# Wide inverse square roots of a two-block transformer kernel: square root and VectorE reciprocal, or ScalarE exp of minus half the logarithm

## What is computed

```python
def rms_norm(x, w):
    xf = x.astype(jnp.float32)
    y = xf * lax.rsqrt(jnp.mean(xf * xf, axis=-1, keepdims=True) + NORM_EPS)
    return (y * w.astype(jnp.float32)).astype(x.dtype)

def l2norm(x):                       # q and k of the delta net
    return x * lax.rsqrt(jnp.sum(x * x, axis=-1, keepdims=True) + NORM_EPS)

# RWKV-7: the removal keys, and the norm of each head's output
kk = kk * lax.rsqrt(jnp.maximum(jnp.sum(kk * kk, axis=-1, keepdims=True), 1e-24))
y = ((y - mu) * lax.rsqrt(var + GN_EPS)).reshape(bsz, s, c) * gn_w + gn_b
```

## Time and profile before

| | |
|---|---|
| median of 3 runs | 2821.63 us |
| profiled execution, its own time | 2820.33 us |
| its span in the trace | 2818.5 us |
| TensorE busy | 2771.2 us (98%) |
| VectorE busy | 2023.7 us (72%) |
| ScalarE busy | 1364.0 us (48%) |
| GpSimd busy | 479.3 us (17%) |
| mean granted TensorE clock | 0.997 of full speed |

### The profile page before, as it was taken

How to read it: one execution, slowest core, us unless ns; L and a number is a source line. 1 busy time by engine, 2 the same in 40 slices (tenths; PEclk the granted TensorE clock), 3 DMA queues, 4 the chain that set the end, 5 groups by cost and what they waited for, 6 DMA issues and landing times.

```text
span 2818.5 us, 42260 instructions
## 1 busy us (share of the span) xinstructions
PE 2771.2 (98%) x16660; PEld 2434.1 (86%) x16660; DVE 2023.7 (72%) x3102; ACT 1364.0 (48%) x2051; POOL 479.3 (17%) x526
## 2 busy tenths in 40 slices
PE   8999999999999999999999999999999999999998
PEld 7888888888888888888888888878998888888887
DVE  7987797776776666656657888878677777667655
ACT  6453455455555445434435545434454444444434
POOL 2211011110111111001102635421111111001101
PEclk9999999999999999999999999999999999999999
DMA  6444333455555555555556534221365555555555
GB/s 227 162 160 159 121 116 132 145 191 188 193 187 190 192 191 191 192 190 193 188 183 199 177 124 133 92 76 53 120 202 191 191 192 189 193 188 194 189 180 164
DMA packets 133396, 474.65 MB, mean 168 GB/s; under 512 B 14800, under 2 KB 15056, under 8 KB 132944
## 3 DMA queue, kind: packets, MB, share of 16 engines
q1 hardware_dynamic: 133200, 471.96, 50.3%
HBM read 469.80 MB, written 2.10 MB: 167 GB/s over the span
## 4 chain that ended last, share of the span: by engine, by line
PE 90%; DVE 5%; ACT 2%; POOL 1%; issue 1%; DMA 0%; SPq 0%; DVEq 0%; ACTq 0%; POOLq 0%
PE ps L899 90%; DVE U L1869 1%; DVE ringl L1869 1%; POOL U L2551 1%; ACT high L1409 1%; PE ps L902 1%; POOL U L2624 0%; ACT U L1409 0%; DVE U L1878 0%; DVE xT L1869 0%; DMA xT<-in_x_dram 0%; DVE hx L1869 0%; DVE U L2067 0%; ACT hr L1409 0%; DVE U L1875 0%
## 5 line engine op out<-in xcount | busy, mean ns | idle before, releaser
L899 PE MATMUL ps<-hr,high 128*128 128x512 f32 x4672 | 1491.4, 397 | 11.8 <-DVE ringl L1869 10.8
L1869 DVE TENSOR_TENSOR ringl<-ring,high 128x1024 fp32r<-128x1024 f32 x888 | 1082.6, 1221 | 435.1 <-ACT high L1409 434.6
L1409 ACT ACTIVATE high<-ring 128x1024 fp32r<-128x1024 f32 x888 | 915.6, 1033 | 601.6 <-PE ps L899 590.7
L899 PEld LDWEIGHTS ps<-hr,ringl 128*128 128x128 f32 x4672 | 879.2, 188 | 192.5 <-issue 1.4
L899 PE MATMUL ps<-hr,ringl 128*128 128x256 f32 x4672 | 924.3, 279 | 0.0
L899 PEld LDWEIGHTS ps<-hr,high 128*128 128x128 f32 x4672 | 717.6, 188 | 21.0 <-issue 15.1
L899 PE MATMUL ps<-yur,high 128*128 128x512 f32 (+1 forms) x2432 | 682.9, 370 | 3.8 <-DVE xT L1869 2.2
L2551 POOL TENSOR_TENSOR U<-U,rs 128x256 f32<-128x256 f32 x292 | 264.5, 906 | 1688.3 <-DVE U L1869 1668.8
L899 PEld LDWEIGHTS ps<-yur,ringl 128*128 128x128 f32 x2176 | 400.0, 188 | 79.6
L1409 ACT ACTIVATE U<-ps 128x256 f32<-128x256 f32 (+3 forms) x481 | 172.8, 371 | 592.0 <-PE ps L899 567.6
L899 PE MATMUL ps<-yur,ringl 128*128 128x256 f32 x2176 | 429.9, 279 | 0.0
(11 more groups left out here) (178 smaller groups left out, 1250.2 us busy)
## 6 DMA issues: line engine op xcount, KB each, us to landing
ring<-in_w_dram SPq DMA_DIRECT2D x862, 512.0 KB, 3.3
ring<-in_w_dram SPq DMA_DIRECT2D x48, 256.0 KB, 3.3
xT<-in_x_dram SPq DMA_DIRECT2D x3, 512.0 KB, 8.1
out_dram<-hx SPq DMA_DIRECT2D x3, 512.0 KB, 2.7
cst<-in_cst_dram SPq DMA_DIRECT2D x1, 1374.5 KB, 12.5
yT<-in_lora_dram SPq DMA_DIRECT2D x1, 1024.0 KB, 7.4
xT<-in_x_dram SPq DMA_DIRECT2D x2, 256.0 KB, 4.5
U<-in_lora_dram SPq DMA_DIRECT2D x1, 512.0 KB, 5.4
```

The lines of the kernel that those rows point to most:

```text
L899: return e.matmul(out, l, r, start=start, stop=stop)
L1409: return e.activation(out, i, ACT.Copy, scale=scale)
L1869: return e.tensor_tensor(out, a, b, op)
```

## The change

Every wide `Sqrt` becomes `Ln`, with the same scale and bias, and is followed on ScalarE by `Exp` with scale -0.5, which is the inverse root; the 256- and 512-column reciprocals of VectorE go. The narrow ones (4 or 2 columns) and the final norm's stay. In the delta net one `Exp` of 1024 columns takes the two halves of q and k together. The planner's tables follow: VectorE's costs drop where a reciprocal went, ScalarE's costs move from the steps that first reloaded a table after a root to the root's own step. GpSimd's scaling waits for ScalarE instead of VectorE.

```diff
-DELTA = [("tanh", ("ACT", 2.8)), ("silu", ("DVE", 1.7)), ("sq", ("ACT", 1.1)), ("ss", ("PE", 1.75), ("ACT", 2.5)),
-         ("rec0", ("DVE", 3.4)), ("rec1", ("DVE", 3.4)), ("nrm", ("DVE", 2.6)), ("gb", ("PE", 0.9), ("ACT", 1.9), ("DVE", 1.4)),
+DELTA = [("tanh", ("ACT", 1.5)), ("silu", ("DVE", 1.7)), ("sq", ("ACT", 1.1)), ("ss", ("PE", 1.75), ("ACT", 4.9)),
+         ("nrm", ("DVE", 2.6)), ("gb", ("PE", 0.9), ("ACT", 0.6), ("DVE", 1.4)),
...
@@ root
-                e.activation(rtmp if tag == "attn_g" else rs, ps[7][:, 0:SEQ], ACT.Sqrt, scale=1.0 / DM, bias=C("eps"))\
-                    .then_inc(mact.sem, mact.inc("rt", tag))
+                r = rtmp if tag == "attn_g" else rs
+                e.activation(r, ps[7][:, 0:SEQ], ACT.Ln, scale=1.0 / DM, bias=C("eps")).then_inc(mact.sem, mact.inc("ln", tag))
+                e.wait_ge(mact.sem, mact.after("ln", tag))
+                e.activation(r, r, ACT.Exp, scale=-0.5).then_inc(mact.sem, mact.inc("rs", tag) if tag != "attn_g" else mact.inc("rt", tag))
@@ deltanet on ScalarE
-                        e.activation(tm[:, 2 * s:2 * s + 2, :], shaped(ps[b][:, :], 2, SEQ), ACT.Sqrt,
+                        e.activation(tm[:, 2 * s:2 * s + 2, :], shaped(ps[b][:, :], 2, SEQ), ACT.Ln,
                                      scale=(128.0, 1.0)[s], bias=C(("eps128", "eps")[s]))\
                             .then_inc(dact.sem, dact.inc("rs", s, g))
+                    e.wait_ge(dact.sem, dact.after("rs", 1, g))
+                    e.activation(tm[:, 0:4, :], tm[:, 0:4, :], ACT.Exp, scale=-0.5).then_inc(dact.sem, dact.inc("inv", g))
@@ rwkv on ScalarE
-                    e.activation(E, E, ACT.Sqrt).then_inc(ac.sem, ac.inc("rk", q))
+                    e.activation(E, E, ACT.Ln).then_inc(ac.sem, ac.inc("lk", q))
+                    e.wait_ge(ac.sem, ac.after("lk", q))
+                    e.activation(E, E, ACT.Exp, scale=-0.5).then_inc(ac.sem, ac.inc("rk", q))
...
-                    e.activation(rs, ps[b][:, 0:256], ACT.Sqrt, scale=1.0 / 64, bias=C("eps64"))\
-                        .then_inc(ac.sem, ac.inc("rs", q))
+                    e.activation(rs, ps[b][:, 0:256], ACT.Ln, scale=1.0 / 64, bias=C("eps64")).then_inc(ac.sem, ac.inc("lv", q))
+                    e.wait_ge(ac.sem, ac.after("lv", q))
+                    e.activation(rs, rs, ACT.Exp, scale=-0.5).then_inc(ac.sem, ac.inc("rs", q))
@@ rwkv on VectorE
                     e.wait_ge(ac.sem, ac.after("rk", q))
-                    e.reciprocal(E, E).then_inc(vc_.sem, vc_.inc())
-                    e.wait_ge(vc_.sem, vc_.last())
                     tt(KK, KK, E, MUL).then_inc(vc_.sem, vc_.inc("nrm", q))
...
                     e.wait_ge(ac.sem, ac.after("rs", q))
-                    e.reciprocal(rs, rs).then_inc(vc_.sem, vc_.inc())
-                    e.wait_ge(vc_.sem, vc_.last())
```

More of the change, by code:

```diff
@@ L1586, in main @@
                             e.wait_ge(mdve.sem, mdve.after("m2"))
-                            e.activation(rs, rs, ACT.Sqrt, scale=1.0 / DM, bias=C("eps")).then_inc(mact.sem, mact.inc("rt2"))
+                            e.activation(rs, rs, ACT.Ln, scale=1.0 / DM, bias=C("eps")).then_inc(mact.sem, mact.inc("ln2"))
+                            e.wait_ge(mact.sem, mact.after("ln2"))
+                            e.activation(rs, rs, ACT.Exp, scale=-0.5).then_inc(mact.sem, mact.inc("rt2"))
                         evac1(u)
@@ L1833, in mla_first @@
                     e.wait_ge(ape.sem, ape.after("ss", c))
-                    e.activation(yT[:, 4, :], ps[7][:, 0:SEQ], ACT.Sqrt, scale=1.0 / 512, bias=C("eps"))\
+                    e.activation(yT[:, 4, :], ps[7][:, 0:SEQ], ACT.Ln, scale=1.0 / 512, bias=C("eps"))\
                         .then_inc(aact.sem, aact.inc("rs", c))
+                    e.wait_ge(aact.sem, aact.after("rs", c))
+                    e.activation(yT[:, 4, :], yT[:, 4, :], ACT.Exp, scale=-0.5).then_inc(aact.sem, aact.inc("inv", c))
                     yield "lat"
@@ L1883, in low_of, with squared_root @@
                 stt(hl[:, t, :], xT[:, t, :], C(tag, t, t + 1), hh[:, t, :], MUL, SUB).then_inc(mdve.sem, mdve.inc("hl", tag, t))
[L1885 to L1889, removed]
+            def squared_root(tag):
                 if tag == "attn_g":
-                    e.wait_ge(mdve.sem, mdve.last())
-                    tt(rs, r, r, MUL).then_inc(mdve.sem, mdve.inc())
+                    e.wait_ge(mact.sem, mact.after("rt", tag))
+                    tt(rs, rtmp, rtmp, MUL).then_inc(mdve.sem, mdve.inc())
                     e.wait_ge(mdve.sem, mdve.last())
@@ L2143, in deltanet @@
                     rota.take()
[L2144 to L2148, removed]
+                    e.wait_ge(dact.sem, dact.after("inv", g))
                     stt(cv[:, 0:4, :], cv[:, 0:4, :], 0.5, tm[:, 0:4, :], MUL, MUL).then_inc(ddve.sem, ddve.inc())
@@ L2207, in deltanet @@
                     yield "z"
-                    e.wait_ge(dact.sem, dact.after("ro", g))
-                    e.reciprocal(sq, sq).then_inc(ddve.sem, ddve.inc())
-                    e.wait_ge(ddve.sem, ddve.last())
+                    e.wait_ge(dact.sem, dact.after("rn", g))
                     stt(oc, oc, C("dn_norm"), sq, MUL, MUL).then_inc(ddve.sem, ddve.inc())
@@ L2494, in mla_first @@
                     yield "lsq"
-                    e.wait_ge(aact.sem, aact.after("rs", c))
+                    e.wait_ge(aact.sem, aact.after("inv", c))
                     r = yT[:, 4, :]
-                    e.reciprocal(r, r).then_inc(adve.sem, adve.inc())
-                    e.wait_ge(adve.sem, adve.last())
                     for k in range(4):
@@ L2557, in evac0 @@
                     if u.i in NORMS:
-                        e.wait_ge(mdve.sem, mdve.after("rs", NORMS[u.i]))
+                        c = mdve if NORMS[u.i] == "attn_g" else mact
+                        e.wait_ge(c.sem, c.after("rs", NORMS[u.i]))
                     d = place_of(u)
```

22 lines of the change are left out of this document (11 added, 11 removed).

## The result

The changed kernel takes 2833.39 us (median of six runs, 2831.05 to 2834.8) beside 2822.09 us for the kernel before on the same chip: ratio 1.0039, 95% interval 1.0026 to 1.0052. It is slower by 11 us; the fastest of its six runs is 6 us above the slowest of the six before. The forecast was 2813.2 us, and its range ended at 2825: wrong in sign, and outside the range.

A forecast was written before the change was run, and what follows sets the result against it. TensorE, busy 2771.2 of 2818.5 us, was taken as the bound, with 26.4 us of idle time in reach. Terms -2.7 - 2.8 - 1.0 - 3.7 + 4.0 - 2.2 gave -8.4 us: median 2813.2 us, range 2804 to 2825.

The forecast's parts named there:

- Item 1: At `up0`: the 3.21 us wait shrinks to 0.5 (-2.7 us) and the clock behind it stays up (-2.8 us).
- 2, other waits to 600 us: Other TensorE waits from 28 to 600 us, 7.7 us, mostly hops between engines: -1 us, between 0 and -3.
- Item 3: Last pair of RWKV heads, before `out1`: 3.7 us of waits all go, as main work now stands behind: -3.7 us.
- Item 4: Run of 155 side matmuls at `out0`: waits of 7.5 to 8 us where 3.8 stood: +4 us, bounds 0 and +12.
- 5, fewer breaks: TensorE main matmuls directly behind side steps: 32 places fewer at 0.07 us each, -2.2 us, between 0 and -3.
- Item 6: Rest of the second mixing stage, 8 us of waits: left as it is, 0 us, between -3 and +4.
- Rival B: Run at `out0` decides: waits double to 16 us, clock falls there once (3 us); slower, 2827 us; chance 16%.
- I cost this at nothing; its cover is ScalarE's idle time: ScalarE's added Exps and table loads, 26.7 us in all, cost nothing: at 1391 of 2818 us it is half idle.
- Rival C: ScalarE's loads cost: 1.38 us more a switch, or late splits; some four late roots, +6 us, 2819 us; chance 5%.
- no drain: On ScalarE a change of table set costs 1.28 us and nothing around it, against the skill page's added 1.38 us.

The follow-up runs named there:

- the one root: The kernel before with only the output norm root of RWKV's seventh pair (q = 6) as Ln and Exp: 2826.5 us, ratio 1.0012.
- the kernel with 0.5 from `uq` on: Changed kernel, planner's threshold for urgent main work 0.5 instead of 1.25 blocks from shortly before the second block's `uq` on: 2828.9 us, ratio 1.0024.

## Why the prediction was wrong, point by point

By its own items, in us, measured from the windows of the two profiled executions:

| item | forecast | measured |
|---|---|---|
| 1, `up0`: wait and clock | -5.5 | -2.8 (1.54 us of waits for 3.21, and 1.7 us of clock for 2.8) |
| 2, other waits to 600 us | -1 | -0.6 |
| 3, last pair of heads | -3.7 | +1.9 (5.6 us idle from 1996 to 2023 us, for 3.7) |
| 4, run at `out0` | +4 | +1.0 idle (4.8 for 3.8), +10.2 clock |
| 5, fewer breaks | -2.2 | -2.8, not measured itself: what is left of TensorE's busy time when the clock's share is taken out (-1.7 when that share is counted on busy time alone) |
| 6, rest of the second stage | 0 | +5.8 idle up to the run at `out0` (13.2 for 7.4), -0.8 between items 4 and 3 |
| sum | -8.4 | +11.9 (the span grew by 12.2; the rest is rounding and the edges of the windows) |

*Item 4 is the step that failed most.* I priced the run by its waits alone ("waits of 2.1, 2.0 and 1.6 us and some six hops of 0.3"). The waits came out smaller, 4.8 us in all. The clock was the cost, 10.2 us, for which the item had no term. Rival B (16%) had the place and the sign, and a time of 2827 us. But most of its 11 us were waits doubled to 16 us, which did not come, and it gave the clock one fall of 3 us, a third of the size: that it came nearest is in part luck. The argument against it was that the worst window before, idle for 3.7 of 11.7 us, "did not lower the clock". It was weak: the other window of the earlier trace rows, with 3.8 us of waits, kept its clock too, and there a single wait 1.7 us longer lowered it. With longest runs of 28 and 29 matmuls the clock there was 1.00, with 40 and 52 it was 0.95, with 155 it was 0.90; but these kernels moved waits elsewhere, so how much of the time the run costs stays open.

*"I cost this at nothing; its cover is ScalarE's idle time" is the second.* An engine that is half idle is no cover for a row that happens to stand in front of what TensorE waits for. I worked out that the root's own latency stays equal at 256 columns, which holds, and stopped there. The equal 1.70 us had moved from VectorE to ScalarE, and ScalarE's list has the copies out of PSUM. Whoever waits there had to be read from the rows behind each root: the wait of 1.61 us before `ps<-U,hx`, released by ScalarE, was in the trace of before. Rival C had the table loads in mind, "four on the path", at 5% and from a worse reason (a drain, or late splits). Its place was wrong, and that its +6 us was about the cost of the instructions, 4 to 5 us, is luck. The rows of the changed kernel show no gap between load and function (load at 1900.90 for 1.28, Exp at 1902.20); the 1.38 us of drain in the Trainium skill, page "ScalarE: Activation LUTs", section "What ACT_TABLE_LOAD costs", are not there, as the forecast said. The same page's section on table sets has one load for Ln and then Exp, from a set with both; the rows above show a load before each.

*Item 3.* Of the 3.7 us that I took for the last pair's, 1.31 were the wait at 2011.15 us ahead of `out1`'s first row, for which the profile names no releaser; 0.89 of it still stand there now (2023.26). The last pair's work did leave the beginning of `out1`, as the lists showed. But "with main work behind it, all of it goes" took for granted that main work has no waits of its own. `out0`'s last blocks, which use two banks, have 0.60 us each for VectorE's addition, which side steps had covered before, and 2.3 us of waits stand between 1998.7 and 2003.1, at the last side steps.

*Item 1* kept 1.0 us more waiting than foreseen (1.54 for 0.5) and a fall of the clock behind 1.03 us. I had taken the length of the wait as the reason for the fall. *Item 6* was costed at zero and is 5 us; the wait of 2.43 us at 1903.07, behind ScalarE's loads, is the largest piece of it; the rest is spread over shorter ones.

What held: 67 loads in ScalarE's list, ScalarE's busy time (1389.9 us for 1391), equal latency of a 256-column root, no drain, and a gain where a root gets shorter. That gain, in the delta net, is 2 us.

What stays open is what exactly brings the clock down. It fell behind waits of 1.03 us (`up0`, changed kernel) and of 3.34 and 3.35 us (the kernels with all instructions in the old order, with RWKV alone and with the one root), and in the long run it stayed low where TensorE did not wait. It did not fall behind 1.61 us. The length of the wait does not decide it: behind the wait of 2.43 us in the changed kernel the clock stayed at 1.00, and in the kernel with 0.5 from `uq` on it fell behind the same wait, 2.41 us there. The first 10 us behind each:

```profile
1903.00:1913.00 10.00, 9.21 (x44) 7.67 (x44) 7.87 (x27) 7.23 (x20) 2.49 (x4) 1.00 0.19 70
```

```profile
1900.00:1910.00 10.00, 8.56 (x34) 6.88 (x36) 7.09 (x22) 6.83 (x18) 3.05 (x4) 0.83 0.23 79
```

So the windows of one execution account for that execution; what a kernel loses by its clock is read from the mean over all its runs. The order's 6 to 7 us are as large as the clock's share by that mean, but no kernel removed the run and nothing else, and the added idle time and the fewer breaks are told apart by windows only. Also not tried: letting ScalarE's copies out of PSUM go ahead of the Exp in RWKV, since a step of its own for the Exp moves the whole list.

## What to carry to other kernels

Moving work from a busy engine to an idle one gained little here, where neither set the pace, and cost time where the work landed in front of something that was waited for: read the target engine's list behind each landing place, above all copies that free a PSUM bank. Where a function takes the result of another function that stands in another set, the load cannot be issued ahead in the list: here it began only when Ln had ended (1900.90 behind 1900.47 and 0.42 us). So in this kernel change roots only where the root itself gets shorter (the delta net, 3.35 us reciprocals), and keep Sqrt and reciprocal at 256 columns. When a planner's order packs the side work into one run, price the clock of that run beside its waits, compare the mean granted clock over all runs, and look at what the main blocks then have to fill their own gaps.

## What the runs showed that I had not expected

- TensorE's granted clock was low while it was busy without a gap: 8.00 of 8.00 us at 0.60, with matmuls of 64, 128 and 256 columns. It was at 0.68 just before, from 1944 to 1950 us, behind a wait of 1.10 us.
- Nearly the same wait in the same stretch had a fall of the clock behind it in one kernel (2.41 us, 0.83) and none in another (2.43 us, 1.00).
- A single wait longer by 1.7 us went with 3 to 4 us in time, and the clock fell behind it (0.52 for six microseconds in the kernel with all of RWKV's roots changed).
- A table load of 1.28 us cost the kernel 0.07 us on average in the old order and 0.15 us in the new one, and a single one with its Exp, in front of a copy that TensorE waited for, 3 to 4 us.
